# Sizes of the three token chunks of a decoder step, and the slot pairs placed beside them

## What is computed

```python
h = rms_norm(x)
q, k, v, u, g_att, g_s5 = split(h @ w_in)
att = rms_norm(diff_attention(q, k, v)) * (1 - lambda_init)   # 8 heads, causal; new tokens read 1024 cached rows
s5y = s5_scan(u)                                              # diagonal state space model
z = gelu(s5y)
s5o = z * sigmoid(z @ w_glu + b_glu)
merged = sigmoid(g_att) * (att @ w_proj_att) + sigmoid(g_s5) * (s5o @ w_proj_s5)
x = x + merged @ w_out
h2 = rms_norm(x)
# PEER: 8 heads; each token picks 16 of 16384 experts by product keys
s1, s2 = (h2 @ w_query) . sub_keys
eidx, gate = top 16 of v1[i] + v2[j], softmax
act = gelu(expert_u[eidx] . h2)
y = rms_norm(x + sum over 8 heads x 16 experts of gate * act * expert_v[eidx])
```

## Time and profile before

| | us |
|---|---|
| median of 3 runs | 4723.79 |
| lowest, highest | 4719.64, 4727.77 |
| the profiled execution | 4727.45 |
| its span | 4725.7 |
| first part | 404 |
| chunk 0 | 455.6 |
| chunk 1 | 938.7 |
| chunk 2 | 1406.7 |
| tail | 1520.7 |

### The profile page before, as it was taken

The page is one execution under the profiler, slowest core; times in us unless marked ns, Lnnn a source line. Parts: engine busy times, 40 slices in busy tenths (PEclk is TensorE's granted clock), DMA queues, the critical chain, the costliest instruction groups (busy, mean ns, idle before and its releaser), DMA issues. The chain is left out here.

```text
span 4725.7 us, 43130 instructions
## 1 busy us (share of the span) xinstructions
PE 3386.6 (72%) x13056; PEld 1917.6 (41%) x13056; DVE 3108.7 (66%) x6859; ACT 1496.0 (32%) x3769; POOL 1344.8 (28%) x1167
## 2 busy tenths in 40 slices
PE   7857878676668476776657848596777777777776
PEld 4636556443434243334446734252222222222221
DVE  6382131577787676878886677696667666666664
ACT  2221130332443213334443333223333333333332
POOL 0000000232223232322122333254444444444443
PEclk9868989888778788888878878799999999999999
DMA  3135325796668797975679997699999999999997
GB/s 124 22 1 125 132 90 194 287 371 250 226 225 329 264 392 297 377 263 204 215 272 405 396 364 318 248 384 377 419 419 416 413 415 413 407 416 403 411 410 311
DMA packets 285978, 1418.38 MB, mean 300 GB/s; under 512 B 47490, under 2 KB 89954, under 8 KB 148642
## 3 DMA queue, kind: packets, MB, share of 16 engines
q0 software_dynamic: 159344, 1129.94, 60.2%
q1 hardware_dynamic: 126018, 285.55, 17.9%
q10 hardware_dynamic: 384, 0.13, 0.0%
HBM read 1371.05 MB, written 42.11 MB: 299 GB/s over the span
## 5 line engine op out<-in xcount | busy, mean ns | idle before, releaser
L895 POOL DMA_INDIRECT arena<-in_uv,arena x1056 | 1276.2, 1209 | 2468.3 <-DVE arena L1006 1578.6
L996 DVE CUSTOM_DVE_ANT_0 arena<-arena 128x1024 f32<-128x1024 f32 x1056 | 1288.9, 1222 | 491.3 <-DMA arena<-in_uv,arena 460.9
L1112 PE MATMUL ps<-arena 128*128 128x512 f32 (+1 forms) x2320 | 1102.2, 621 | 415.3 <-ACT arena L1081 415.3
L648 PE MATMUL ps<-arena 128*128 128x256 f32 (+2 forms) x3456 | 1129.6, 488 | 229.8 <-DMA arena<-in_w_stat 59.9
L648 PEld LDWEIGHTS ps<-arena 128*128 128x128 f32 x3456 | 695.4, 204 | 629.0 <-issue 445.6
L1112 PEld LDWEIGHTS ps<-arena 128*128 128x128 f32 (+1 forms) x2320 | 420.4, 190 | 1096.5 <-ACT arena L1081 640.9
L1062 ACT ACTIVATE arena<-arena 128x2 f32<-128x2 f32 x528 | 107.2, 203 | 1691.1 <-DVE arena L996 1690.6
L1006 DVE SCALAR_TENSOR_TENSOR arena<-arena 128x1024 f32<-128x1024 f32 x476 | 609.1, 1280 | 41.5 <-ACT arena L1071 41.5
L1071 ACT ACTIVATE arena<-arena 128x1 f32<-128x1 f32 x1056 | 253.4, 287 | 17.9 <-ACT arena L1062 0.8
L1062 ACT ACT_TABLE_LOAD x157 | 201.4, 1283 | 4.7 <-issue 1.9
L1081 ACT ACTIVATE arena<-ident,arena 128x128 f32<-128x128 f32 x548 | 190.2, 394 | 9.4 <-PE ps L1112 0.4
(11 more groups left out here) (248 smaller groups left out, 3323.2 us busy)
## 6 DMA issues: line engine op xcount, KB each, us to landing
arena<-in_w_stat SPq DMA_DIRECT2D x216, 512.0 KB
arena<-in_cache_k SPq DMA_DIRECT2D x64, 512.0 KB
arena<-in_cache_v SPq DMA_DIRECT2D x64, 512.0 KB
arena<-in_w_mov SPq DMA_DIRECT2D x14, 2048.0 KB, 10.6
arena<-in_uv,arena POOLq DMA_INDIRECT x1056
arena<-in_x SPq DMA_DIRECT2D x16, 512.0 KB, 8.6
arena<-scr_s POOLq DMA_DIRECT2D x64, 128.0 KB
scr_s<-arena SPq DMA_DIRECT2D x16, 384.0 KB
```

The source lines that it names most:

```text
L648: last = nc.tensor.matmul(ps[:, bank, 0:w], wbuf[m % NWB][:, kc * P:(kc + 1) * P], moving[:, kc, :], start=(kc == 0), stop=(kc == KC - 1))
L895: pool.indirect_dma_start(ring[s % RING], None, dr["uv"], bass.IndirectOffsetOnAxis(ap=idx[:, g % 4, j:j + 1], axis=0)).then_inc(row_in[s ...
L996: nc.vector.tensor_tensor_reduce(ring[s % RING][:, 0:D], ring[s % RING][:, 0:D], h2r[:, b % 2, :], 1.0, 0.0, ALU.mult, ALU.add, act_in[:, ...
L1112: last = nc.tensor.matmul(ps[0:m, 4 * (b % 2) + c, :], diag[:, n % 4, 0:m], ring[s % RING][:, D + 512 * c:D + 512 * (c + 1)], start=start, ...
```

## The change

The limits of the chunks move by one block, from (2, 3, 4) blocks to (3, 3, 3), where the last block of each last chunk is the one of 32 tokens. So `W` is 384, 384 and 288 in place of 256, 384 and 416. The table places 8, 16, 10, 32, 0, 16, 8 and 20 pairs beside the stages of chunk 1 (110 in place of 96) and 7, 14, 8, 24, 40, 14, 6 and 16 beside those of chunk 2 (129 in place of 142). `PAIRS_FRONT` becomes 239 in place of 238.

```diff
-        CHUNKS = ((0, 2), (2, 5), (5, NB))
+        CHUNKS = ((0, 3), (3, 6), (6, NB))
         STAGES = ("glu", "s5", "v", "att", "dec", "ga", "out", "query")
         PAIR_PLAN = ((0, 0, 0, 0, 0, 0, 0, 0),
-                     (7, 14, 9, 27, 0, 14, 7, 18),
-                     (8, 15, 10, 28, 40, 15, 8, 18))
+                     (8, 16, 10, 32, 0, 16, 8, 20),
+                     (7, 14, 8, 24, 40, 14, 6, 16))
```

## The result

The changed kernel takes 4821.17 us (median of 4 runs, 4819.69 to 4827.91) against 4721.72 us of before in the same session: a ratio of 1.0213, 95% interval 1.0196 to 1.0231. It is slower by 99.5 us, where +146 was forecast; the time lies inside the range of 4790 to 4925. The profiled execution has a span of 4826.1 us, 100.4 more than before.

The account below looks back on a forecast made before the run. Chunk 0 was taken as PE-bound, chunks 1 and 2 mostly ended by DVE's pairs, the tail DMA-bound. Terms +202 (chunk 0), +92 (chunk 1), -143 (chunk 2), -5 (tail) sum to +146: 4870 us, range 4790 to 4925.

Parts of the forecast that it names:

- The PE-bound rival: Chunk 2: PE is the bound, so the change pays back what it takes; 4673 us, faster; chance 0.05.
- The rival of a large fixed part in each tile: Chunk 0: part of each matmul is fixed, so tiles grow 0.6 us, not 1.81; 4784 us; chance 0.04.
- nothing fixed: Stationary tiles of eight products: 0.0141 us a token at 256, 384 and 416 tokens, nothing gained by a wider tile.
- The dearer rival: Chunk 0 and added pairs cost more: attention 27.6 us a head, half clock, DMA pushed over; 4934 us; chance 0.10.
- the table did place what its numbers say: Rival: only 119 pairs beside chunk 2, ten moving to the tail, -59 + 52 us; no chance given.
- the signs named in advance: Chunk 0 about 657 us, its s5 86, chunk 1 1030; most chunk 2 stages 9 to 16 us shorter, longer PE waits.
- 24 us a head: Chunk 0 attention: 16.0 us a head becomes 24, the third block hiding only behind the q tile; +64 us.
- the tile's growth: Chunk 0 matmul stages: each tile 1.81 us longer, from 3.62 at 256 tokens to 5.43 at 384.
- 5.9 us a pair, since PE already waits: Chunk 1's glu, s5, v, ga and out: seven added pairs at DVE's 5.9 us each, +41 us.
- 0.55 us a tile: Chunk 1 attention: DVE's price for three more 128-key tiles in each of 8 heads, 13 us.
- the forecast's 4.2 and its 7 us: Chunk 2 attention: DVE's own part falls 4.2 us a head; narrower tiles and one hand-over less give about 7 more.
- Pairs are nearly neutral wherever they stand: A pair beside a DVE-bound stage costs 5.9 us and saves 5.2 in the tail; uncovered matmul time matters.

Follow-up runs that it names:

- the first experiment: New chunk limits (384, 384, 288 tokens) with the old table of 96 and 142 pairs, against the kernel before: 4822.01 us against 4723.05, ratio 1.0203.
- The halved kernels: Pairs beside chunks 1 and 2 with DVE's part, gathers or both halved: 4548.5, 4632.3, 4357.1 us on old limits; 4658.1, 4739.4, 4407.1 on new.

## Why the prediction was right, and where it was off

**The mechanism** was right: chunk 0's growth has no cover and is paid in full; chunk 2 does not return it, because pairs end its stages. The kernels with the new limits alone and those without pairs show both halves of it: +166 to +172 in chunk 0 with pairs or without, and 190 back in chunk 2 without pairs, 90.5 with the same pairs, while PE's waits there grew. The PE-bound rival (4673) is out: its condition, PE's list longer than first tiles plus pairs, does not hold in the glu, s5 and ga stages of either chunk, where PE stood still for 25 to 31 us at the end. The rival of a large fixed part in each tile (growth of 0.6 us) is out too. PE in order of time in the attention of chunk 0, around a q tile, against the earlier trace rows:

```profile
625.53 0.44 PE L1417 MATMUL ps<-ident,arena 128*128 128x128 f32 x2 [0.76 <-DVE arena L1537]
625.81 5.33 PE L648 MATMUL ps<-arena 128*128 128x384 f32 x16
630.97 0.61 PE L1432 MATMUL ps<-arena 128*128 128x128 f32 x4
631.42 0.49 PE L1417 MATMUL ps<-ident,arena 128*128 128x128 f32 x3
632.49 0.94 PE L1432 MATMUL ps<-arena 128*128 128x128 f32 x6 [0.58 <-ACT arena L1479]
```

The tile takes 5.33 us against 3.62 at 256 tokens, 1.47 times; PE's busy time in the s5 stage of chunk 0 grew 1.48 times (55.90 to 82.75 us). So "nothing fixed" was nearly right, not exactly. The dearer rival did not come either, and the table did place what its numbers say (289 pairs in the tail).

Of the signs named in advance, s5 of chunk 0 (83.8 us), chunk 1 (1027.8), the tail (5.2 a pair), both attentions and s5 of chunk 1 (+9.6) came out on the side of the forecast. PE's waits at the stages' ends became longer in the main (25 to 31 us in glu, s5 and ga), but not before out of chunk 2 (25.2 for 27.1). The stages of chunk 2 did not keep to "9 to 16 us shorter": only v (11.4) and ga (12.8) did, while glu lost 3.9, s5 8.4, dec 5.6 and query 19.1. The whole stands 49 us below the forecast of 4870; 31 of them are chunk 0, which took 626.4 us for about 657 and came out at the lower end of its bounds (170), and 12 are chunk 2.

**Chunk 0, +171 for +202.** Three terms were too large. The attention, taken at 24 us a head between 19.6 and 27.6, measured 21.6. DVE's row once a head, in chunks 0 and 2, against the earlier trace rows:

```profile
L1570 DVE TENSOR_TENSOR arena<-arena x8: 557/558/559, 636.0 to 787.4; 128x384 f32<-128x384 f32 x8
...
L1570 DVE TENSOR_TENSOR arena<-arena x8: 424/424/427, 2343.2 to 2590.7; 128x256 f32<-128x256 f32 x8
```

(787.4 - 636.0) / 7 = 21.6: of the 5.6 us that a head grew, 3.6 are its two wider tiles, so the third query block hides but for 2 us. The step that failed was that the q tile of 5.4 us would not be enough to hide behind. In the rows of PE above the third block's transposes (L1417 x3) follow the q tile and the products behind it without a wait: DVE had finished that block's probabilities (L1537, 628.67 to 629.29 us) while the q tile still ran, until 631.14. That makes 7 x 2.4 = 16.8 us less; the start and the last head took 0.8 more than forecast. The second term is the tile's growth, 1.81 us from two single rows: it is 26.2 / 16 = 1.64 by the stages. I had taken the 384-token row from a tile that began after an idle time, and a mean over a stage would have been the better row; over the 56 tiles outside attention that is 9 us. Third, the query stage of before held 5.5 us that did not come again: PE waited 3.75 us for a tile's weights and ran that tile in 5.38 in place of 3.62 us. I carried them along as if they were work.

**Chunk 1, +89 for +92,** right with a price that was too high. "5.9 us a pair, since PE already waits" treated DVE's list as the only end, although the page's DMA row had nines inside the chunks, not only behind the last one. By the first experiment a pair there costs 5.3, and by the one with 20 fewer 3.9 over both chunks. The halved kernels say why: in glu, s5 and ga DVE's list and the transfers are nearly equal, in the query stage the transfers end it, and only attention, v and out are DVE's. Attention was forecast at +43 and grew by 39.9. The longer rows cost 14.8 us for 13; their price of 0.55 us a tile should have read 0.59, (17.8 - 12.5) / 9. The two errors partly cancelled.

**Chunk 2, -155 for -143.** Here too the pair's price was too high, and the error ran against the one of chunk 1 (13 fewer against 14 more), so that it left hardly a trace in the sum. Attention fell by 75.7 for 64: a head is (2590.7 - 2343.2) / 7 = 35.4 us for 44.5. The new limits alone (first experiment) had brought it to (2546.3 - 2279.9) / 7 = 38.1, 6.4 us less, where the forecast's 4.2 and its 7 us over eight heads make 5.1; the four pairs are the other 2.7, forecast at 2.9. DVE waited 27.3 us for the k and q tiles in this stage, 40.4 before. So the narrower tiles and the hand-over less were worth more than I gave them. dec fell by 5.6 where nothing was forecast, query by 19.1 for 16; glu by 3.9 for 9.

**"Pairs are nearly neutral wherever they stand"** holds for exchange between chunks (the new table cost 16.6 us on the old limits and nothing on the new), not for their number: the 238 pairs beside the chunks save 575 us against none, and 20 fewer lose 28. The last 20 gave back 3.9 us each for 5.2 saved; the 238 as a whole cost 2.8 each (chunks 1 and 2 are 657.9 us shorter without them). So the first pairs of a stage fall into waits, and the last ones cost nearer to what they save.

In chunk 2 ga goes like s5 (124.7 us as it is, 5.6 less with DVE's part halved, 2.7 with the gathers, 21.9 with both), and v and out follow DVE's list (4.5 and 14.0 less with DVE's part halved, 0.5 less and 1.0 more with the gathers). What stays open is what ends the stages once both are halved, and so where the last 50 us of loss come from.

## What to carry to other kernels

When work is split into chunks and a second kind of work fills the gaps of all but the first, keep the first chunk small: here each column in it was paid in full, and the later chunk returned only what its cover left uncovered (about half). A first chunk of one block was not tried. A waiting engine at the end of a stage says that it is not the limit, but not which of the others is; halve each candidate alone and both together before pricing. Take a unit price as a mean over a stage without waits, not from one row.

## What the runs showed of the hardware

The granted clock of PE fell in chunk 2 where the tiles became narrower: 0.87 to 0.78 in glu, 0.80 to 0.76 in attention (for the s5 stage the row of after shows 0.81). PE stood still longer before: the first 6.4 us of chunk 2's s5 stage had 0.73 after 18.5 us without work and now have 0.61 after 26.1 us, and the 9 us behind them 1.00 in both. A tile of 288 columns that took 4.15 us at full clock took 6.96 in the query stage, where the stretch from 3282.8 to 3286.2 us was granted 0.50, the lower level of 1.2 GHz. What the slower first tiles cost was not separated. In chunk 0, which has no pairs beside it, the s5 stage of back-to-back tiles had 1.00 at 256 and at 384 tokens alike. A DVE dot product over 512 columns took 688 ns against 1220 over 1024, an addition 747 against 1281: halving the columns left 56% and 58%.
